# A two-block transformer kernel: side-by-side rounds behind two norms, and the token norms' inverse roots as a power on GpSimd

## What is computed

```python
def conformer_conv(h, w_in, b_in, w_dw, b_dw, ln_g, ln_b, w_out, b_out):
    ...                                   # gated input product, 31-tap depthwise convolution
    u = layer_norm(u, ln_g, ln_b)         # mean and variance over the 2048 channels of a token
    u = jax.nn.silu(u)
    return u @ w_out + b_out              # "out2": 2048 x 2048

u = conformer_conv(rms_norm_2(h, ...), ...)
h = h + rms_norm_2(u, norm_mix_post)      # root of the mean square over a token's channels
u = swiglu(rms_norm_2(h, norm_ffn_pre), w_gate, w_up, w_down)   # "glu0" to "glu2", "back0" to "back2"
h = h + rms_norm_2(u, norm_ffn_post)      # the last norm, then the output is stored
```

## Time and profile before

| | |
|---|---|
| median of 3 runs | 2555.91 us (2555.3 to 2556.78) |
| the profiled execution | 2555.95 us, span 2554.1 us |
| TensorE busy | 2530.6 us, 99% of the span |
| VectorE, ScalarE, GpSimd busy | 1736.2, 1263.8, 456.6 us |
| mean granted TensorE clock | 0.995 of 2.4 GHz |

### The profile page before, as it was taken

The page is one execution under the profiler, slowest core; times in us unless marked ns, Lnnn a source line. Parts: engine busy times, 40 slices in busy tenths (PEclk is TensorE's granted clock), DMA queues, the critical chain, the costliest instruction groups (busy, mean ns, idle before and its releaser), DMA issues.

```text
span 2554.1 us, 42977 instructions
## 1 busy us (share of the span) xinstructions
PE 2530.6 (99%) x14675; PEld 2232.7 (87%) x14675; DVE 1736.2 (68%) x2096; ACT 1263.8 (49%) x1589; POOL 456.6 (18%) x290
## 2 busy tenths in 40 slices
PE   9999999999999999999999999999999999999998
PEld 8888888888888888888888899988788888888887
DVE  7577875677765665665667889984766556655665
ACT  5456555554544444444445554555644444444444
POOL 5034410002100000000011368872400000000001
PEclk9999999999999999999999999999999999999999
DMA  7655565665656666566555565536466666656554
GB/s 230 189 168 178 161 180 186 197 190 180 190 187 191 189 189 189 181 197 189 185 185 189 184 171 163 162 103 200 149 194 198 199 183 189 188 190 189 181 182 163
DMA packets 475057, 466.38 MB, mean 183 GB/s; under 512 B 14521, under 2 KB 449203, under 8 KB 474803
## 3 DMA queue, kind: packets, MB, share of 16 engines
q1 hardware_dynamic: 474432, 464.97, 59.0%
q10 hardware_dynamic: 546, 0.38, 0.1%
HBM read 463.20 MB, written 2.10 MB: 182 GB/s over the span
## 4 chain that ended last, share of the span: by engine, by line
PE 96%; DVE 2%; ACT 1%; issue 1%; DMA 0%; DVEq 0%; ACTq 0%
PE gp L430 50%; PE gp L433 23%; PE gp L730 3%; PE gp L729 3%; PE gp L731 3%; PE gp L439 3%; PE gp L648 2%; PE gp L650 2%; PE gp L649 2%; DVE wlo L1334 1%; PE xp L666 1%; PE xp L695 0%; ACT whi L792 0%; DMA work<-in_x 0%; PE gp L617 0%
## 5 line engine op out<-in xcount | busy, mean ns | idle before, releaser
L1334 DVE TENSOR_TENSOR wlo<-stage,whi 128x1024 fp32r<-128x1024 f32 x809 | 1023.3, 1279 | 672.0 <-ACT whi L792 666.3
L430 PE MATMUL gp<-A,whi 128*128 128x512 f32 x4224 | 1406.9, 394 | 5.9 <-DVE A L1807 2.9
L792 ACT ACTIVATE whi<-stage 128x1024 fp32r<-128x1024 f32 x874 | 914.8, 1057 | 952.3 <-PE gp L433 622.3
L433 PE MATMUL gp<-A,wlo 128*128 128x256 f32 x3456 | 970.9, 281 | 0.0
L430 PEld LDWEIGHTS gp<-A,whi 128*128 128x128 f32 x4224 | 788.5, 188 | 181.0 <-issue 6.9
L433 PEld LDWEIGHTS gp<-A,wlo 128*128 128x128 f32 x3456 | 653.0, 189 | 0.0
L430 PE MATMUL gp<-B,whi 128*128 128x512 f32 x1536 | 534.6, 393 | 0.7 <-issue 0.7
L433 PE MATMUL gp<-B,wlo 128*128 128x256 f32 x1536 | 429.5, 280 | 0.0
L430 PEld LDWEIGHTS gp<-B,whi 128*128 128x128 f32 x1536 | 287.6, 187 | 66.0 <-issue 1.1
L433 PEld LDWEIGHTS gp<-B,wlo 128*128 128x128 f32 x1536 | 290.0, 189 | 0.0
L1985 POOL TENSOR_TENSOR sq<-r 128x512 f32 (+1 forms) x32 | 43.0, 1344 | 806.0 <-DVE r L1599 756.0
(11 more groups left out here) (312 smaller groups left out, 1943.5 us busy)
## 6 DMA issues: line engine op xcount, KB each, us to landing
stage<-in_w_in SPq DMA_DIRECT2D x160, 512.0 KB, 4.4
stage<-in_w_up SPq DMA_DIRECT2D x128, 512.0 KB, 3.8
stage<-in_w_down SPq DMA_DIRECT2D x128, 512.0 KB, 3.7
stage<-in_ffn_w_gate SPq DMA_DIRECT2D x88, 512.0 KB, 4.4
stage<-in_ffn_w_up SPq DMA_DIRECT2D x88, 512.0 KB, 4.3
stage<-in_ffn_w_down SPq DMA_DIRECT2D x88, 512.0 KB, 4.3
stage<-in_conv_w_in SPq DMA_DIRECT2D x64, 512.0 KB, 4.0
stage<-in_w_o SPq DMA_DIRECT2D x32, 512.0 KB, 4.6
```

Source lines behind the costliest of these rows:

```text
L430: nc.tensor.matmul(bank.rearrange("p (a t) -> p a t", a=2), hi, both_parts(M, kt), start=first, stop=False)
L433: done = nc.tensor.matmul(bank[:, T:2 * T], lo, M[:, kt, 0:T], start=False, stop=last)
L792: nc.scalar.activation(unit_homes(n, slot)[0], stage[:, slot, :], ACT.Copy).then_inc(hi_ready, 1)
L1334: nc.vector.tensor_tensor(lo, stage[:, slot, :], hi.bitcast(F32), ALU.subtract).then_inc(lo_ready, 1)
```

## The change

1. **Walk side by side.** In the first body of out2 and of glu0 TensorE alternates between the two column blocks k-tile by k-tile (the last unit of each is done whole, block after block). The eight units come in the order block 0, block 1, block 0, ...; loads and conversions follow that order, and units 4 and 5 are converted in the middle of the norm's chain.
2. **Inverse roots of the token norms** by a GpSimd `tensor_tensor` with the power operation and an exponent of -1/2, in both norms and in the last one. Reciprocal and ScalarE's square root go. Scale factors and epsilon move into other operations.
3. **Diagonals** are made by VectorE.
4. **Fillers** (`keep_busy`, matmuls on ones) before and behind both spreads.
5. **First tiles** of the second norm are kept in `r`; the copies go.
6. **Sums of the pre norm**: `column_sums(5)` from behind unit 1 to behind unit 4 of glu0's second body; `variance`, `glu_scale`, `glu_product`, `glu_low` from units 2, 4, 5, 6 to 5, 6, 7, 7.
7. **Table loads** of ScalarE for the square roots go; the one for Silu moves ahead of the last squares.
8. **Mean subtraction** of the first pair of tiles is cut in two.
9. **The tail**: VectorE makes all four blocks of the second token half.

```diff
+            def side_by_side(phase, M, ready):          # TensorE
...
+                for u in range(3):
+                    for k in range(4):
+                        ready_for(4 * u + k)
+                        for j in range(2):
+                            block(u, j, k)
+                for j in range(2):
+                    for k in range(4):
+                        if j == 0:
+                            ready_for(12 + k)
+                        block(3, j, k)
...
+            keep_busy(2, gp[:, 3, :])
             spread(0, ln_rstd)
-            body("out2", 0, A, (ln_ready, 0, 4), single=True)
+            keep_busy(4, gp[:, 3, :])
+            side_by_side("out2", A, (ln_ready, 0))
...
             token_sums(0, lambda t: 3 * t, [acc[:, 0:T], acc[:, T:2 * T]])
+            keep_busy(2, gp[:, 0, :])
...
             token_sums(0, lambda t: 3 * t + 2, [root[:, T:2 * T]]).then_inc(stat_ready, 1)
+            keep_busy(3, gp[:, 0, :])
             spread(1, post_rstd)
-            body("glu0", 0, A, (r_ready, 48, 4), {3: [lambda: pe.wait_ge(first_kept, 2)]}, single=True)
-            body("glu0", 1, A, (r_ready, 48, 4), {1: [lambda: column_sums(5)]})
+            keep_busy(4, gp[:, 0, :])
+            side_by_side("glu0", A, (r_ready, 48))
+            body("glu0", 1, A, (r_ready, 48, 4), {4: [lambda: column_sums(5)]})
```

```diff
-            nc.scalar.activation(table_ahead[:, 1:2], ones_r[:, 0:1].bitcast(F32), ACT.Sqrt)
+            nc.scalar.activation(table_ahead[:, 2:3], ones_r[:, 0:1].bitcast(F32), ACT.Silu)
             last_squares_of_v(15)
...
-            root_of_tokens(4, 3)
-            diagonal_of_tokens(4)
-            nc.scalar.activation(table_ahead[:, 2:3], ones_r[:, 0:1].bitcast(F32), ACT.Silu)
...
+                if c == 3:
+                    hi_of("out2", 4, 5)
...
-            glu(0, 1, units={2: [lambda: root_of(6)], 5: [lambda: glu_sigmoid(0, F[:, 0:2, :])],
-                             6: [lambda: glu_high(0, 0, F[:, 0:2, :])]})
+            glu(0, 1, units={5: [lambda: root_of(4)], 6: [lambda: glu_sigmoid(0, F[:, 0:2, :])],
+                             7: [lambda: glu_high(0, 0, F[:, 0:2, :])]})
```

```diff
+            def rstd_of_tokens(n, value, w, factor):     # VectorE
+                y = tok[:, 2, :]
+                dve.wait_ge(rsqrt_made, n + 1)
+                nc.vector.scalar_tensor_tensor(w, y, -1.0, y, ALU.mult, ALU.mult).then_inc(stat_refined, 1)
...
+                nc.vector.tensor_tensor(w, value, w, ALU.mult).then_inc(stat_refined, 1)
...
+                nc.vector.scalar_tensor_tensor(tok[:, 3, :], w, 3.0, y, ALU.add, ALU.mult).then_inc(stat_rstd, 1)
...
+                for t in range(2):
+                    nc.vector.tensor_scalar(token_diag[:, t * P:t * P + P], ident[:], tok[:, 3, t:t + 1], factor,
+                                            ALU.mult, ALU.mult).then_inc(diag_made, 1)
                 dve.wait_ge(rstd_spread, n + 1)
...
+            dve.wait_ge(gained, 1)
+            first_add(0)
             post_scale(1)
...
             first_low(0)
+            first_add(1)
             post_scale(2)
             first_low(1)
...
-            glu(0, 1, units={2: [lambda: variance(6, 6, RMS_EPS)], 4: [lambda: glu_scale(0, first)],
-                             5: [lambda: glu_product(0, first)], 6: [lambda: glu_low(0, 0, first)]})
+            glu(0, 1, units={5: [lambda: variance(4, 6, RMS_EPS)], 6: [lambda: glu_scale(0, first)],
+                             7: [lambda: glu_product(0, first), lambda: glu_low(0, 0, first)]})
```

```diff
             take_lo(n0 + RING + 63, 3)                   # GpSimd
+            def rsqrt_of(value, o, signal, *ready):
+                pool.wait_ge(*ready)
+                nc.gpsimd.tensor_tensor(o, value, minus_half.broadcast_to([P, o.shape[-1]]), ALU.pow).then_inc(signal, 1)
+
+            pool.wait_ge(half_set, 1)
+            rsqrt_of(tok[:, 1, :], tok[:, 2, :], rsqrt_made, ln_var, 1)
             pool.wait_ge(mean_ready, 1)
...
             take_lo(at["glu0"][1] + RING - 1, RING - 1)
+            rsqrt_of(tok[:, 0, :], tok[:, 2, :], rsqrt_made, sums_folded, 2)
...
             take_gain(slice(0, 1), 3 * WIDE, WIDE, (part_added, 1))
+            rsqrt_of(tok[:, 0, 0:1], tok[:, 1, 0:1], token_root, token_var, 1)
             take_gain(slice(1, 2), 3 * WIDE, T, (part_added, 2))
             take_gain(slice(1, 2), 3 * WIDE + T, T, (part_added, 3))
-            pool.wait_ge(scaled, 1)
-            o = GT[:, 1, 2 * WIDE:3 * WIDE]
-            nc.gpsimd.tensor_tensor(o, o, rt[:, 1, 2 * WIDE:3 * WIDE], ALU.add).then_inc(pool_out, 1)
+            rsqrt_of(tok[:, 0, 1:2], tok[:, 1, 1:2], token_root, token_var, 2)
```

More of the change, by code:

```diff
@@ L179, in two_block_kernel @@
         rt = work[:, KT * T:KT * T + 2 * D].rearrange("p (a d) -> p a d", a=2)
[L180 removed]
+        table_ahead, minus_half = work[:, 12800:12803], work[:, 12803:12804]
         post_rstd = xp[:, 1, 0:T]
[L182 removed]
         token_diag = var[:, 0:T]
@@ L320, in panels, with pairs, side_by_side @@
                         panel(n0 + 8 * it + 4 * j, 0, w, row0, KT, col0 + (2 * it + j) * HPW)
-            def pairs(phase, wa, ca, wb, cb, its):
+            def pairs(phase, wa, ca, wb, cb, its, first_it=0):
                 n0 = at[phase][1]
-                with sp.Fori(0, its) as it:
+                with sp.Fori(first_it, its) as it:
                     panel(n0 + 8 * it, 0, wa, 0, KT, ca + it * HPW)
                     panel(n0 + 8 * it + 4, 0, wb, 0, KT, cb + it * HPW)
+            def side_by_side(phase, wa, ca, wb, cb):
+                n0 = at[phase][1]
+                for u in range(4):
+                    load(n0 + 2 * u, 2 * u % RING, wa[:, 4 * u:4 * u + 4, ca:ca + HPW])
+                    load(n0 + 2 * u + 1, (2 * u + 1) % RING, wb[:, 4 * u:4 * u + 4, cb:cb + HPW])
             def half_panels(phase, w):
@@ L1196, in out2 @@
                     take_cross(hp0 + 2 * it + j, j, n + 4, bias=lambda m: col("b_out", 4 * it + 2 * j + m))
-                    if not first or j:
-                        apply_gain(U, "mix_post", 4, 2 * it + j - 1, 1)
-            out2(0, True)
+                    apply_gain(U, "mix_post", 4, 2 * it + j - 1, 1)
             with act.Fori(1, 3) as it:
@@ L1237, in _ @@
                 nc.scalar.activation(part(A, 0, 2 * h, 2), gained_r(h), ACT.Copy).then_inc(r_hi, 2)
-            for m in range(2):
-                nc.scalar.activation(r[:, m, :], first_r[m], ACT.Copy).then_inc(first_kept, 1)
+                if h == 3:
+                    hi_of("glu0", 4, 5)
             def post_squares(h):
-                if h == 0:
-                    act.wait_ge(first_kept, 2)
                 nc.scalar.activation(U[:, 2 * h:2 * h + 2, :], r[:, 2 * h:2 * h + 2, :], ACT.Square).then_inc(post_sq, 1)
@@ L1773, in _ @@
                 ln_low(2 * c - 4, ln_home(c - 2))
-            dve.wait_ge(lo_ready, at["out2"][1] + RING)
+                if c == 5:
+                    dve.wait_ge(lo_ready, at["out2"][1] + RING)
+                    lo_of("out2", 4, 5)
             hp0, n0 = at["out2"]
-            with dve.Fori(0, 3) as it:
+            lo_of("out2", 6, 7, 8, 9)
+            add_up(hp0, 0, U[:, 0:2, :])
+            lo_of("out2", 10)
+            add_up(hp0 + 1, 1, U[:, 2:4, :])
+            lo_of("out2", 11)
+            with dve.Fori(1, 3) as it:
                 for j in range(2):
@@ L1821, in _ @@
                 post_low(h - 2)
-            dve.wait_ge(lo_ready, at["glu0"][1] + RING)
+                if h == 5:
+                    dve.wait_ge(lo_ready, at["glu0"][1] + RING)
+                    lo_of("glu0", 4, 5)
             def glu_scale(c, four):
@@ L2153, in _ @@
                 nc.gpsimd.tensor_tensor(two(acc), two(acc), U[:, 2 * h:2 * h + 2, :], ALU.add).then_inc(acc_ready, 1)
+            for t in range(2):
+                last = nc.gpsimd.memset(square_sums[:, t, 0:1], 4.0 * RMS_EPS)
+            last.then_inc(half_set, 1)
             pool.wait_ge(gain_spread, 16)
```

184 lines of the change are left out of this document (103 added, 81 removed).

## The result

The changed kernel takes 2563.91 us (median of 10 runs) against 2556.81 us of the kernel before, run beside it: ratio 1.0029, interval 1.0021 to 1.0037. Nine of its ten runs took 2561.67 to 2565.61 us; the tenth took 5093.97 at the full granted clock, which nothing here explains, and the ratio leaves it out. The forecast was 2558.6, its range ended at 2562.8. So the kernel became slower, as forecast, but by 7.1 us instead of 2.7, and the time lies outside the range. Of the 5.3 us between the time and the forecast 0.9 are no part of the change: the forecast stood on the 2555.91 of the kernel before, and that kernel took 2556.81 this time. A difference of 7.1 us is larger than the 0.2% (5.1 us) that can be told from no change. The profiled execution took 2562.53 us at a span of 2560.7; that is 6.6 more than the profiled span before.

What follows compares the result with a forecast made beforehand. TensorE's own work and its gaps were taken as the bound. First norm -2.6, second norm -0.2, glu0 sums +6.0 and tail -0.5 gave +2.7 on 2555.91, so 2558.6 us; range 2552.8 to 2562.8.

Steps and rivals of the forecast that it cites:

- First norm, the refining and the diagonals: First norm: three VectorE refining steps of 0.2 us, diagonals 0.3, so spread and first out2 matmul start 0.6 earlier.
- The prediction's own tail: After the last matmul: VectorE takes four blocks in 2.74 us with GpSimd silent, ending at 2550.8 instead of 2551.3: -0.5.
- Rival 3, the dear power: GpSimd's power is slow, paid at second norm, tail and partly first norm; at 2.35 us each, 2564.1; chance 0.09.
- rival 5: Change does what it says everywhere: clock held in first norm, no wait in glu0; -4.5, 2551.5 us; chance 0.05.
- The power: GpSimd power of two elements replacing reciprocal and ScalarE root in the norms: taken as 0.3 us, no row showing it.
- The 6 us for a first call: First norm: first call of a freshly loaded GpSimd routine pays about 6 us; estimate then 2564; chance 0.03.
- The clock at the first norm: Dense work behind the first spread: fillers leave 2 us at the low clock instead of 6.1, winning 2.0 us.
- The table load: Silu load in the first norm, 1.28 us: holds nobody up; by the page, its removal would win up to 1.3 more.
- The queue behind the low half: Second norm: power waits behind GpSimd's 2.35 us low half of glu0's unit 3; first matmul +1.4.
- The clock's share: Second norm: clock falls, but half of the 2.1 us lost at the low clock is won back: -1.1.
- a new wait of 0.82: Sign of being wrong: a new wait of TensorE inside the side-by-side walks; no size given.
- A wait of 3.3 us for a low half in the third body: glu0's third iteration: TensorE waits 3.5 us for VectorE's low half, clock fall adds 2.5; together +6.0.

Runs made afterwards that it cites:

- the kernel of four edits: Changed kernel with first-norm refining operands in PSUM and ScalarE diagonals, low half on VectorE, gating in glu0's third body, second-norm scaled tile in PSUM: 2551.54 us, ratio 0.9982.

## Why the prediction was wrong, and where it was right

**First norm, the refining and the diagonals: the step that failed.** The prediction took "three steps of 0.2", without bounds, and 0.3 for the diagonals, between 0.17 and 0.69, and put the first matmul 0.6 earlier. They took 2.49 and 2.47, and it came 3.6 later. Its rows were of instructions with another neighbour or another home: it read what the steps cost without reading where their operands lay, and it kept GpSimd's subtractions in the sum only as suppliers of tiles, at 1.24 a pair, not as neighbours. The code of the two kernels shows that the operands move (`by_token(3)`, in PSUM, to `tok`, in SBUF), which the list of the change leaves out. The prediction's own tail had the effect in its numbers: it counted four blocks at 2.74 "with GpSimd silent" where three had taken 3.08 beside GpSimd, and did not ask the same of the first norm. The kernel before also has the mechanism in plain sight, in a place that the prediction didn't read. Groups by shape between 1816 and 1840 us: count, busy us, mean ns:

```profile
L1334 DVE TENSOR_TENSOR wlo<-stage,whi 128x1024 fp32r<-128x1024 f32 x10 | 17.8, 1806 | 2.5 <-ACT whi L792 2.4
...
L2153 POOL TENSOR_TENSOR acc<-acc,work 128x512 f32<-128x512 f32 x8 | 16.6, 2074 | 4.2 <-ACT work L1244 3.2
```

The low half takes 1.81 on average there, 1.23 elsewhere, and GpSimd's 512-column sum 2.07, where the subtraction of that size takes 1.24. The Trainium skill (SBUF — State Buffer, Who interferes with whom) states the rule: a VectorE instruction with two SBUF inputs contends with a GpSimd one that reads SBUF, `tensor_scalar` can too, and the later one is blocked for the whole instruction. The traces agree where they bear on it: VectorE's small steps took 0.17 with a PSUM input and 0.65 to 2.22 with two inputs in SBUF, the diagonals are `tensor_scalar`, and a GpSimd sum that started 0.1 us behind a VectorE instruction (1808.97 in the changed kernel) took 1.54 instead of 1.26. Whether a GpSimd instruction that only writes SBUF is left alone, no run here shows. None of the rivals held this case. Rival 3, the dear power, would have given a time close to the measured one at the same place, but it isn't the cause: the power took 0.71. (The sum of rival 5 is 0.2 off: -3.6 - 0.2 - 0.5 is -4.3, not -4.5. Nothing hangs on it.)

**The power.** Taken as 0.3, it took 0.71 for two numbers a lane and 0.56 for one, nearer to the small row than to the far one, as argued. From the variance to the first refining step it is 1.12 us (1700.13 to 1701.25), where reciprocal and ScalarE's root had taken 1.05 (1700.38 to 1701.43). So this replacement wins nothing. The first power of the program was the one of 0.71. The 6 us for a first call, which the prediction took from the Trainium skill (GPSIMD Engine Reference, 2.1 Instruction dispatch), have no trace here.

**The clock at the first norm.** 2.0 forecast, 2.3 measured in B, but for a reason only half given. The forecast rested on fillers; the runs show that fillers give time only together with the walk (0.0 without it, 3.0 with it). The walk has no term of its own in the sum, and that was wrong in the same measure: at the high clock it is the walk that keeps TensorE supplied (B is 5.75 with it and 7.76 without it, both at a granted clock of 1.00).

**The table load.** It stood beside the wait for scaled values before, and with its removal A gained 0.25 at best (7.49 against 7.74). It was hidden, as the prediction said. The 2.66 us with a drain, which the prediction set against it, don't show: from the end of the diagonals at 1702.72 over the load to ScalarE's next instruction at 1704.04 it was 1.32 us.

**Second norm.** The queue behind the low half was right: the power started at 1804.41 behind 2.34 us, and the first matmul came 1.65 later after the sums, forecast 1.4. The small gap went, -0.52, forecast -0.5. The clock's share was half of the forecast (-0.45 for -1.1), because a new wait of 0.82 stood inside the walk, which the prediction had named as what would show it wrong: the second tile's sum took 1.07 beside GpSimd. In the kernel of four edits, with that sum in PSUM, D is 6.51, which is 1.07 below the kernel before and near the forecast share.

**glu0.** A wait of 3.3 us for a low half in the third body (forecast 3.5), and 1.7 for the clock (forecast 2.5, from the mean of two earlier restarts). The place and the size of the wait were right. The prediction counted that the first gating stands ahead of the next iteration's low half, and the two runs show that this is the part that matters: the sums and all of the gating but its low part one unit earlier took 0.65 off the wait, the gating in the third body all of it.

**The tail.** Forecast -0.5, measured 0.0. Four blocks took 2.74 where three had taken 3.08, as forecast, -0.3. The road from VectorE's last sum to the first block grew from 2.39 to 2.61 by the power.

**The sum.** With A at its measured size and the rest as forecast the sum would have been 2.7 + 4.2 = +6.9, against 6.6 between the profiles; that the remaining misses nearly cancel (glu0 -1.1, the other norm and the tail +1.4, the clock of the first norm -0.3) is luck. The range was too narrow because its upper end held only cases of the power and the clock; an instruction of 0.2 us had no bound of its own.

## What to carry to other kernels

Before moving small VectorE work from PSUM to SBUF, look at what GpSimd does beside it: with two inputs in SBUF the price of a small instruction is not its own size but that of GpSimd's, once for each instruction in the chain. Keep one operand in PSUM, give the copy-like step to ScalarE, or let GpSimd start later; putting its long instruction "behind" the chain doesn't help if it starts while the chain runs. And fillers are worth their name only where the dense work behind them isn't already limited by those who feed it: ask what TensorE would wait for at the high clock.

## What the runs showed of the hardware that I had not expected

VectorE instructions of 128x2 elements with two inputs in SBUF lasted 0.25, 0.65, 1.19 and 2.22 us beside GpSimd instructions of 0.28, 0.70, 1.24 and 2.34, 0.16 beside none, and 0.17 beside those of 0.70 with one input in PSUM. A power of two elements a lane on GpSimd takes 0.71 us, one element 0.56. With the same 3.26 us of waiting ahead of it, the dense work ran at the low clock for 3.0 us in one profiled execution and 5.7 in another, which made 1.2 us; what decided between them stays open.
